# The order of the first solve product, the block rows and the value products in the RWKV units of a two-block kernel

## The reference

```
def rwkv7_scan(r, w, k, v, a, b):
    def step(state, xs):
        r_t, w_t, k_t, v_t, a_t, b_t = xs
        sa = jnp.einsum('bhvk,bhk->bhv', state, a_t)
        state = state * w_t[:, :, None, :] + sa[..., None] * b_t[:, :, None, :] + v_t[..., None] * k_t[:, :, None, :]
        return state, jnp.einsum('bhvk,bhk->bhv', state, r_t)
...
wkv = rwkv7_scan(r, w_f, k, v, a_vec, b_vec) + flip_t(
    rwkv7_scan(flip_t(r), flip_t(w_b), flip_t(k), flip_t(v), flip_t(a_vec), flip_t(b_vec)))
```

## Time and profile before

| | us |
|---|---|
| median of 3 runs | 1573.28 |
| lowest and highest | 1570.07, 1573.85 |
| the profiled execution | 1580.58 |
| its span, first to last instruction | 1579.3 |
| TensorE busy | 1496.2 (95%) |
| VectorE busy | 1047.0 (66%) |
| ScalarE busy | 788.3 (50%) |

### The profile page before, as it was taken

One profiled execution on the slowest core, in us unless ns is written; L12 is line 12 of the kernel. 1 busy time (PEld: TensorE's weight loads), 2 busy tenths in 40 slices (PEclk: granted clock), 3 DMA queues, 4 the chain that ended last, 5 costly groups with the idle time before them and its releaser, 6 DMA issues.

```text
span 1579.3 us, 27437 instructions
## 1 busy us (share of the span) xinstructions
PE 1496.2 (95%) x11810; PEld 1321.9 (84%) x11810; DVE 1047.0 (66%) x1758; ACT 788.3 (50%) x1342; POOL 52.0 (3%) x58
## 2 busy tenths in 40 slices
PE   7999999999999998999999999899889989999998
PEld 7888898899989988988899989888778878885566
DVE  5577665655565776647555586856866768767877
ACT  4656544544454465445444466433542446856335
POOL 0001011000000010120000000000000000000000
PEclk9999998999999999989999998999879799999999
DMA  8554344475555553434655554210001267441133
GB/s 271 181 177 149 107 134 147 147 243 187 187 186 154 190 160 108 134 107 156 207 199 187 187 192 154 87 55 1 2 2 36 75 215 203 143 128 38 54 128 132
DMA packets 151190, 219.13 MB, mean 139 GB/s; under 512 B 6228, under 2 KB 110684, under 8 KB 150428
## 3 DMA queue, kind: packets, MB, share of 16 engines
q1 hardware_dynamic: 151068, 217.37, 42.5%
HBM read 216.29 MB, written 1.06 MB: 138 GB/s over the span
## 4 chain that ended last, share of the span: by engine, by line
PE 74%; DVE 15%; ACT 7%; DMA 2%; issue 1%; SPq 1%; DVEq 0%
PE bank L396 19%; PE bank L398 18%; PE bank L397 18%; DVE weights_low L372 4%; PE bank L3764 2%; PE bank L2201 1%; DMA place<-w_in_dram 1%; ACT weights_high L359 1%; PE bank L2159 1%; PE bank L898 1%; PE bank L3774 1%; PE bank L3725 1%; PE bank L3785 1%; DVE place L1240 1%; PE bank L2096 1%
## 5 line engine op out<-in xcount | busy, mean ns | idle before, releaser
L372 DVE TENSOR_TENSOR weights_low<-place,weights_high 128x1024 fp32r<-128x1024 f32 (+2 forms) x387 | 449.2, 1204 | 169.9 <-ACT weights_high L359 169.2
L359 ACT ACTIVATE weights_high<-place 128x1024 fp32r<-128x1024 f32 (+2 forms) x387 | 378.8, 1033 | 125.4 <-DMA place<-w_down_dram 40.7
L396 PE MATMUL bank<-hT_high,weights_high 128*128 128x256 f32 x1152 | 326.4, 283 | 2.5 <-DVE hT_low L493 1.5
L397 PE MATMUL bank<-hT_low,weights_high 128*128 128x256 f32 x1152 | 320.5, 278 | 0.0
L398 PE MATMUL bank<-hT_high,weights_low 128*128 128x256 f32 x1152 | 320.3, 278 | 0.0
L396 PEld LDWEIGHTS bank<-hT_high,weights_high 128*128 128x128 f32 x1152 | 218.0, 189 | 6.5 <-DVE hT_low L493 2.2
L397 PEld LDWEIGHTS bank<-hT_low,weights_high 128*128 128x128 f32 x1152 | 217.8, 189 | 0.6
L398 PEld LDWEIGHTS bank<-hT_high,weights_low 128*128 128x128 f32 x1152 | 217.7, 189 | 0.0
L398 PE MATMUL bank<-weights_high,branchT_low 128*128 128x512 f32 x256 | 100.8, 394 | 0.0
L397 PE MATMUL bank<-weights_low,branchT_high 128*128 128x512 f32 x256 | 100.5, 393 | 0.0
L396 PE MATMUL bank<-weights_high,branchT_high 128*128 128x512 f32 x256 | 99.8, 390 | 0.3
(11 more groups left out here) (441 smaller groups left out, 3160.7 us busy)
## 6 DMA issues: line engine op xcount, KB each, us to landing
place<-w_in_dram SPq DMA_DIRECT2D x48, 1024.0 KB, 5.3
place<-w_up_dram SPq DMA_DIRECT2D x32, 1024.0 KB, 5.3
place<-w_down_dram SPq DMA_DIRECT2D x32, 1024.0 KB, 4.9
place<-even_w_in_dram SPq DMA_DIRECT2D x17, 1024.0 KB, 5.2
place<-w_out_dram SPq DMA_DIRECT2D x16, 1024.0 KB, 5.0
place<-odd_w_in_dram SPq DMA_DIRECT2D x16, 1024.0 KB, 5.7
place<-w_branch_dram SPq DMA_DIRECT2D x12, 1024.0 KB, 5.0
place<-ple_gate_dram SPq DMA_DIRECT2D x8, 1024.0 KB, 5.3
```

What stands on the lines that cost most here:

```text
L359: nc.scalar.activation(high[:, lo:hi], self.raw[p % SLOTS][:, lo:hi], ACT.Copy).then_inc(*A("high", p, j))
L372: nc.vector.tensor_tensor(low[:, lo:hi], self.raw[p % SLOTS][:, lo:hi], high[:, lo:hi].bitcast(FP32), ALU.subtract).then_inc(*V())
L396: nc.tensor.matmul(out, left[0], right[0], start=first, stop=False)
L397: nc.tensor.matmul(out, left[0], right[1], start=False, stop=False)
```

## The change

In the first and third unit the first solve product comes ahead of the next unit's rows on TensorE, and its copy ahead of the quarters (`quads_scalar`) on ScalarE; the rows' copy moves behind the quarters. In the second unit the rows keep their place ahead of the first solve product, but `o_values_tensor` moves from in front of them to behind the first solve product. On ScalarE the first unit's last part of the decay moves behind the second solve copy, with a wait of ScalarE on itself ahead of the transposes' copies, since they write where the decay read. On VectorE the second decay product moves behind the subtraction of the third solve product. The fourth unit keeps its order. No instruction is added or removed.

```diff
@@ rwkv_tensor
                 pairs[n].finish()
                 corner_tensor(k, v, tag, tag[1])
                 a_sums_tensor(k, e, n - 1)
-                o_values_tensor(k, e, n - 1)
@@
+def first_calls(step):
+    calls = iter((step,))
+    def call(n=1):
+        next(calls, lambda: None)()
+    return call
@@ solved_tensor
         following, then = ("rk", *RK_UNITS[n + 1]), e.inverse_rk[(n + 1) % 2]
+    if n == 1:
         rows_tensor(k, e, then, following)
     def after_first():
         if step == 0:
+            rows_tensor(k, e, then, following)
             turned("db", e.dbT[d])
         elif pairs:
+            o_values_tensor(k, e, n)
             pairs()
@@ rwkv_vector
-            for _ in decay:
-                pass
+            if n == 1:
+                next(decay)
             substitute_vector(k, unit, step_tag, RK_UNITS[n][0])
             solve_vector(k, tag, split(e.U, 8, 64), 8, 64, lambda n=1: None)
+            if n == 1:
+                for _ in decay:
+                    pass
@@ rwkv_scalar
-            if more:
+            def of_unit():
                 quads_scalar(k, unit, step_tag, ("M_masked", *step_tag))
                 if n == 2:
                     rhs_scalar(k, e, tag)
-            turn = second_calls(lambda: k.turn_scalar(("mixedT", 0), e.close.hT, KT, 1))
+                rows_scalar(k, unit, step_tag)
+            if n == 2:
+                of_unit()
+            between = second_calls(lambda: k.turn_scalar(("mixedT", 0), e.close.hT, KT, 1))
+            if n == 2:
+                between = lambda: None
+            elif more:
+                between = first_calls(of_unit)
+            solve_scalar(k, tag, split(e.U, 8, 64), split(e.work, 8, 64), 8, 64, between)
             if n == 1:
                 next(decay, None)
-            if more:
-                rows_scalar(k, unit, step_tag)
-            solve_scalar(k, tag, split(e.U, 8, 64), split(e.work, 8, 64), 8, 64, (lambda: None) if more else turn)
+                A.wait_ge(A)
```

## The result

| | before | after |
|---|---|---|
| median, us | 1573.28 | 1586.93 |
| lowest, us | 1570.07 | 1578.78 |
| ratio (95% interval) | | 1.0068 (1.0049 to 1.0087) |
| the profiled execution | 1580.58 | 1588.21 |
| its span | 1579.3 | 1586.9 |

The changed kernel is slower, by 0.5 to 0.9%. Its executions differ by their mean granted clock: four took 1585.4 to 1589.0 us at 0.955 to 0.960, two 1578.8 and 1579.8 us at 0.965 and 0.966. A seventh, in a slower state, took 1605.36 us at 0.912: the median of 1586.93 counts it (without it, 1586.19), the ratio does not.

A forecast was written before the change was run, and what follows sets the result against it. TensorE, busy 95% of the span and at half clock in two stretches, was taken as the bound; order terms -1.8, +1.15 and +0.95 gave +0.3, the lost clock +8: from 1573.3 to 1581.3 us, range 1569 to 1590.

The forecast's parts named there:

- The clock in the second unit: New 1.3 us pause ahead of the second unit's rows loses TensorE's upper clock: +8 us, from 6 to 16; chance 0.55.
- The second unit without the clock: Second unit's new order at the upper clock, with TensorE pausing 1.3 to 1.4 us ahead of the rows: +1.15 us.
- The first unit: First solve product fills TensorE's idle time behind the corner product in the first unit, at the lower clock: -1.8 us.
- The third unit: TensorE waits 0.95 us for the corner's copy in the third unit: +0.95 us, between 0.9 and 2.6.
- The dearer case: Third unit at the upper clock, where the substitution would arrive last: up to 2.6 us.
- The order alone: Rival: second unit keeps its clock in most executions and the three order terms cancel: 1573.6 us, chance 0.28.
- The first unit keeping the clock: Rival: the solve product shortens the first unit's idle time, so its clock holds: faster, 1568 us, chance 0.12.

The follow-up runs named there:

- e1: The kernel before with only the second unit's value products moved behind the first solve product: 1587.30 us, ratio 1.0077.
- e4: The kernel before in its old order, with VectorE repeating block work so that TensorE pauses ahead of the second unit's rows: 1586.29 us, ratio 1.0075.
- e3: The changed kernel with nine unused 128x128 products filling TensorE's wait ahead of the second unit's rows: 1579.99 us, ratio 1.0034.

## Why the prediction was right, and where not

*Forecast.* 1581.3 us in a range of 1569 to 1590, slower as the likeliest case; measured 1586.93. The profiled execution was forecast at 1588.6 and took 1588.21. The mechanism came out as forecast, and the size was taken too low: I had taken 8 us from a span of 6 to 16, while the medians moved by 13.7 us, the ratio says 10.7, and the two profiles differ by 13.4 within the units. I had taken less because I expected executions of both kinds in the medians; two of six took 1579 us. That the profiled execution hit its forecast to 0.4 us is luck: of the 13.4, 2.8 were offset by a lead that this execution had before the units and 3.0 by less low clock behind them, neither of which the change made. For the same reason the 7.3 us by which the profiled execution of before lay above its median could not be carried over to after, where it is 1.3.

*The clock in the second unit* was the term that decided. Forecast: lost some 1.5 us into what follows the pause, in most executions. It went 1.0 us into the rows (the low stretch begins at 1193.8). That it did so in four of the six executions, and in five of six with the values alone, is judged by their times and mean clocks; only the profiled ones show the place. From the a_sums to the output products I had 1.15 + some 7 us for what lies ahead of them; 8.45 were measured. Behind them, 10.4 us were to stretch by 6 to 8 if the clock stayed low to the third unit's new state. It came back sooner, among the pairs of heads with 256 columns, so this part cost about 2.9 us, and 1.27 of these are the third unit's value products, in which the clock fell again sooner than before.

*The second unit without the clock* was forecast at +1.15. With the pause filled it is 15.33 - 13.22 = 2.1, of which 0.6 are the fill's own excess: about 1.5. A part of the error is in the way from the third product to the output products, which I took as 1.7 us; it takes 1.92 with the pause filled, and 1.95 in the earlier trace rows. The pause, 1.30, and its releaser were as forecast.

*The first unit* was forecast at -1.8. Measured from the corner's copy it gave -2.02, but that agreement is luck. The term stood on a clock that falls behind the corner product and leaves 2.74 us idle. In the profile of after, and in five of the six others without fills in the first unit, the clock was lost sooner, the idle time had shrunk to some 0.7 us by the old order (e1, e4), and the swap gained 0.35 us in the profile of after and nothing where the clock was lost ahead of all value products. Only e3's profile has the forecast case, and there the gain is 2.1 us. The rest of the term held: the substitution ended 10.7 us after the corner's copy (forecast 10.8), ahead of its user at 1172.21. The decay moved behind the second solve copy was covered: ScalarE had copied the transposes by 1173.7, and the new state needed them at 1176.7. The wait of ScalarE on itself is not visible.

*The third unit* was forecast at +0.95 and gave +0.76, with a wait of 0.88 us for the corner's copy; the substitution ended at 1240.06, 0.6 us ahead of its user, "just covered", as forecast for the lower clock. The dearer case, up to 2.6 at the upper clock by the substitution, is what the kernels with fills show: 1.5 us, with a wait of 1.80.

*The rivals.* The order alone may be what two of the six executions show, by their clocks of 0.965 and 0.966; at 1578.8 and 1579.8 us they lie above the 1572.8 to 1575.5 of that rival, and no profile shows them. The first unit keeping the clock did not happen without fills. Its price was partly right: with fills the output products came 10.0 us after the corner's copy, where that rival had 11.5. But the reading behind it fell. I laid the first fall to the 2.74 us of idle time behind the corner. In the profile of after the clock was low from 1156.2 on, during the value products and 4.7 us ahead of the end of the corner's copy, in the old order with the values moved from 1154.9. There the solve product in the idle time came too late to save it; in the profile of before it may have been the idle time. What TensorE did ahead of these falls was to wait 1.70 us for VectorE at the first unit's second level, and then to sit idle 1.16 us (after) and 1.43 (e1) in the wave of 32x32 products that follows; before, which lost the clock later, has 1.70 and 0.88. The prediction had not counted these.

The Trainium skill (TensorE: Matmul & The Clock Gate, Part 1, the section on oscillation) lays losses of the clock to idle stretches much longer than 1.3 us, by which the second unit should have kept it. The measurement decides: the clock was lost behind 1.30 us of idle time (clock 0.50 from 1194 to 1217), and held when the same place was filled. Small tiles surround the pause in this kernel, and no run here separates their part from the pause's.

## What to carry to other kernels

On an engine whose clock can drop, a wait of a microsecond is not priced at its length: here 1.3 us of idle time among short products on small tiles cost 8 to 14 us in the median. Before work that fills such a wait is moved away, look at the granted clock on both sides of the place, and either leave the filler or put unused products of the wait's length there, in all such waits of the stretch, since filling one or two of several left the fall at another. What a reorder saves depends on the clock too: the idle time that the first swap was to fill was 2.74 us in one execution and 0.7 in others, because the work ahead of it had slowed down. Compare two profiles from a point ahead of where their clocks part. And do not carry the distance between one profiled execution and the median over to another kernel: the profiled one may sit in a different share of low-clock stretches than the runs it stands for.

## What was unexpected of the hardware

The time of an execution follows its mean granted clock closely, within one kernel too: 1579 us at 0.966 and 1588 at 0.957 in the changed kernel, 1563.6 to 1569.5 at 0.976 to 0.981 and 1579.5 to 1584.2 at 0.968 to 0.971 in the swaps with fills. One kernel thus has two or more groups of times on one core; where they part is not shown, since each kernel has one profiled execution. And unused work at the right places made the kernel faster: in the swaps with fills L287, most of it added, takes 10.4 us of TensorE's time between 1150 and 1262, and the fourth unit's output products still come 9.5 us earlier, counted from the L2096 products ahead of the units (100.92 us against 110.44 before). The kernel before with fills, which lost its clock in the fourth unit, has 110.29.
